# Two rotary half turns by DMA exchange in SBUF in place of permutation products, in a two-layer four-mixer block

## The reference, cut to what matters

```python
def apply_rope(x, cos, sin):
    half = cos.shape[-1]
    r = 2 * half
    ...
    x1, x2, rest = x[..., :half], x[..., half:r], x[..., r:]
    return jnp.concatenate([x1 * c - x2 * s, x2 * c + x1 * s, rest], axis=-1)
...
qb = apply_rope(qb, cos_p, sin_p) * DSWA_DH ** -0.5     # b, local attention
kb = apply_rope(kb, cos_p, sin_p)
...
qd = apply_rope(qd.reshape(B, S, RET_HEADS, RET_DK), cos_r, sin_r)    # d, retention
kd = apply_rope(kd.reshape(B, S, RET_HEADS, RET_DK), cos_r, sin_r) * RET_DK ** -0.5
```

## Time and profile before

| what | value |
|---|---|
| median of 3 runs (lowest, highest) | 2326.5 us (2324.55, 2334.76) |
| span of the profiled execution | 2324.0 us |
| TensorE busy | 2297.4 us, 99% |
| weight load of TensorE busy | 1870.2 us, 80% |
| VectorE, ACT, GpSimd busy | 851.0, 751.4, 1282.2 us |
| DMA | 196.72 MB, mean 85 GB/s |

### The profile page before, as it was taken

One profiled execution on the slowest core, in us unless ns is written; L12 is line 12 of the kernel. 1 busy time (PEld: TensorE's weight loads), 2 busy tenths in 40 slices (PEclk: granted clock), 3 DMA queues, 4 the chain that ended last, 5 costly groups with the idle time before them and its releaser, 6 DMA issues.

```text
span 2324.0 us, 31844 instructions
## 1 busy us (share of the span) xinstructions
PE 2297.4 (99%) x13054; PEld 1870.2 (80%) x13054; DVE 851.0 (37%) x1350; ACT 751.4 (32%) x1505; POOL 1282.2 (55%) x732
## 2 busy tenths in 40 slices
PE   8999999999999999999999999999999999999998
PEld 7788877877877888888887888778778778888887
DVE  4543225334445521123355430254243445112233
ACT  5633226213035321122355341451230544112121
POOL 5513654554554566677655136546555445666874
PEclk9999999999999999999999999999999999999999
DMA  4311331322221243322222113213222213333331
GB/s 151 91 38 47 95 87 46 118 82 86 75 89 52 92 124 92 100 94 97 82 79 85 36 54 93 73 60 115 84 88 84 74 60 101 108 100 94 97 100 64
DMA packets 105904, 196.72 MB, mean 85 GB/s; under 512 B 8480, under 2 KB 18848, under 8 KB 105504
## 3 DMA queue, kind: packets, MB, share of 16 engines
q1 hardware_dynamic: 104608, 188.40, 26.8%
q10 hardware_dynamic: 1152, 6.29, 0.8%
HBM read 192.57 MB, written 2.10 MB: 84 GB/s over the span
## 4 chain that ended last, share of the span: by engine, by line
PE 96%; ACT 2%; DVE 2%; issue 1%; DMA 0%; DVEq 0%; ACTq 0%
PE big L1722 71%; PE mix L1722 9%; PE mix L1867 5%; PE big L2074 1%; PE mix L2042 1%; PE mix L2144 1%; PE mix L2053 1%; PE mix L1827 1%; PE mix L2272 0%; PE mix L2225 0%; PE mix L1781 0%; ACT o_hi L618 0%; PE mix L2209 0%; PE mix L2195 0%; PE mix L1999 0%
## 5 line engine op out<-in xcount | busy, mean ns | idle before, releaser
L583 POOL TENSOR_TENSOR ring_lo<-stage,ring_hi 128x1024 fp32r<-128x1024 f32 (+3 forms) x364 | 912.4, 2507 | 30.4
L581 POOL TENSOR_SCALAR ring_hi<-stage 128x1024 fp32r<-128x1024 f32 (+3 forms) x364 | 371.3, 1020 | 987.9 <-PE big L1722 906.6
L1722 PE MATMUL big<-h_hi,ring_hi 128*128 128x512 f32 (+1 forms) x1888 | 720.6, 382 | 3.0 <-DVE h_lo L1173 1.8
L1722 PE MATMUL big<-h_hi,ring_lo 128*128 128x512 f32 (+1 forms) x1888 | 709.3, 376 | 0.0
L1722 PE MATMUL big<-h_lo,ring_hi 128*128 128x512 f32 (+1 forms) x1888 | 709.2, 376 | 0.0
L1722 PEld LDWEIGHTS big<-h_hi,ring_hi 128*128 128x128 f32 x1888 | 355.4, 188 | 75.1 <-issue 8.6
L1722 PEld LDWEIGHTS big<-h_lo,ring_hi 128*128 128x128 f32 x1888 | 355.4, 188 | 65.7
L1722 PEld LDWEIGHTS big<-h_hi,ring_lo 128*128 128x128 f32 x1888 | 355.7, 188 | 62.9 <-issue 1.4
L1663 DVE TENSOR_TENSOR h_lo<-scr,h_hi 128x1024 fp32r<-128x1024 f32 x64 | 84.7, 1323 | 248.5 <-ACT h_hi L1091 248.5
L1722 PE MATMUL big<-ring_hi,h_hi 128*128 128x512 f32 x448 | 174.2, 390 | 0.0
L1722 PE MATMUL big<-ring_lo,h_hi 128*128 128x512 f32 x448 | 174.1, 390 | 0.0
(11 more groups left out here) (304 smaller groups left out, 2758.0 us busy)
## 6 DMA issues: line engine op xcount, KB each, us to landing
stage<-in_w_in SPq DMA_DIRECT2D x168, 512.0 KB, 3.5
stage<-in_w_mlp_in SPq DMA_DIRECT2D x64, 512.0 KB, 3.7
stage<-in_w_mlp_out SPq DMA_DIRECT2D x64, 512.0 KB, 3.6
stage<-in_w_o SPq DMA_DIRECT2D x16, 512.0 KB, 3.6
stage<-in_w_br_a SPq DMA_DIRECT2D x8, 512.0 KB, 3.6
stage<-in_w_br_c SPq DMA_DIRECT2D x8, 512.0 KB, 3.6
stage<-in_w_br_d SPq DMA_DIRECT2D x8, 512.0 KB, 3.6
stage<-in_w_br_b SPq DMA_DIRECT2D x8, 512.0 KB, 3.6
```

The lines of the kernel that those rows point to most:

```text
L581: nc.gpsimd.tensor_scalar(rH[jw][0:pp, r, 0:kk, 0:job.n], w, 1.0, 0.0, ALU.mult, ALU.add).then_inc(sem("w_hi"), 1)
L583: nc.gpsimd.tensor_tensor(rL[jw][0:pp, r, 0:kk, 0:job.n], w, f32(rH[jw][0:pp, r, 0:kk, 0:job.n]), ALU.subtract).then_inc(sem("w_ready"), 1)
L1722: ins_ = MM(o_, a_, r_, start=s0, stop=s1)
```

## The change

Both rotations no longer use TensorE. The tiles are copied as they are to SBUF (`dX`, `bX`). `swapped` then issues four DMAs from ACT's queue which copy SBUF to SBUF, from `dX` to `dY` (four tiles at once, 32 rows each) and from `bX` to `bY` (8 rows each; bq0's four tiles at once, then bk0's, then bqk's one). They exchange the two halves of every head. The minus sign stands in the sine table. VectorE multiplies the copy by cosine, the exchanged copy by sine, and adds. In local attention the cosine product still reads the PSUM bank and frees it; the rows of `bY` that no DMA writes are zeroed once a layer by a memset on VectorE. `bX` and `bY` take the place of `o_hi` and `o_lo`. The matrices leave the constants, and the 13 rotations of a layer leave the order of the `mix` banks.

```diff
-        [... sel, rotation(8), rotation(32), -one(c <= p), ...], 1)
+        [... sel, -one(c <= p), ...], 1)
...
-        for b in (0, half):
+        for b, sign in ((0, -1.0), (half, 1.0)):
             cos[b:b + half] = np.cos(ang.astype(np.float64))
-            sin[b:b + half] = np.sin(ang.astype(np.float64))
+            sin[b:b + half] = sign * np.sin(ang.astype(np.float64))
...
+ROPE_LAST = (3, 7, 8)
+def rope_at(i):
+    return i % 4 if i < 8 else 4
...
+        o_at = nc.sbuf_base - 4 * 10 * S
+        b_raw = nc.alloc_sbuf_tensor_at("b_raw", [P, 10 * S], F32, offset=o_at)
-        dX, dY = sview(MB + 4096, 4), sview(MB + 10240, 2)
+        dX, dY = sview(MB + 4096, 4), sview(MB + 9216, 4)
+        bX, bY = (b_raw[:, 5 * S * i:5 * S * (i + 1)].rearrange("p (k w) -> p k w", w=S) for i in range(2))
...
+            def swapped(dst, src, tiles, half):
+                for b in range(0, P, DH):
+                    for r0, r1 in ((b, b + half), (b + half, b)):
+                        act.dma_start(dst[r0:r0 + half, tiles, :], src[r1:r1 + half, tiles, :]).then_inc(sem("exchanged"), 16)
...
             for i in range(4):
                 big_freed(act, ("dqk", i))
-                exact_hi(("drot", i), dX[:, i, :])
+            swapped(dY, dX, slice(0, 4), DH // 2)
...
-            def rope_hi(i):
+            def rope_raw(i):
                 ps = big_wait(act, WROPE[i])
-                if i >= 5:
-                    mix_wait(act, ("brot", i - 5))
-                A(oH[:, i % 5, :], ps[:, :], ACT.Copy).then_inc(sem("b_rhi"), 1)
+                if 4 <= i < 8:
+                    act.wait_ge(*upto("b_rope", i - 3))
+                A(bX[:, rope_at(i), :], ps[:, :], ACT.Copy).then_inc(sem("b_raw"), 1)
+                if i in ROPE_LAST:
+                    act.wait_ge(*upto("b_raw", i + 1))
+                    if i == 8:
+                        act.wait_ge(*upto("b_rope", 5))
+                    act.wait_ge(*upto("b_zero", 1))
+                    swapped(bY, bX, slice(0, 4) if i < 8 else slice(4, 5), 8)
...
             dve.wait_ge(*upto("tab", 16))
+            dve.wait_ge(*upto("exchanged", 64))
             for i in range(4):
-                rope(i, ("drot", i), ...)
+                TT(dX[:, i, :], dX[:, i, :], dTab[:, TRC:TRC + S], ALU.mult).then_inc(sem("d_rp"), 1)
+                TT(dY[:, i, :], dY[:, i, :], dTab[:, TRS:TRS + S], ALU.mult).then_inc(sem("d_rp"), 1)
+                dve.wait_ge(*upto("d_rp", 2 * i + 2))
+                TT(dQK[:, i, :], dX[:, i, :], dY[:, i, :], ALU.add).then_inc(sem("d_rope"), 1)
...
-            def rope_parts(i):
+            def rope_cos(i):
                 ps, key = big_wait(dve, WROPE[i]), WROPE[i]
-                dve.wait_ge(*upto("b_rhi", i + 1))
-                TT(oL[:, i % 5, :], ps[:, :], f32(oH[:, i % 5, :]), ALU.subtract).then_inc(sem("b_rlo"), 1)
+                dve.wait_ge(*upto("b_raw", i + 1))
                 if i >= 6:
-                    mix_freed(dve, ("brot", i - 6))
+                    dve.wait_ge(*upto("b_rope", i - 5))
                 big_free(TT(bR[:, i % 6, :], ps[:, :], bTab[:, 0:S], ALU.mult), key)
             def rope_sum(i):
-                key, t1 = ("brot", i), bR[:, i % 6, :]
-                ps = mix_wait(dve, key)
-                TT(ps[:, :], ps[:, :], bTab[:, S:2 * S], ALU.mult).then_inc(sem("b_rp"), 1)
+                t1, t2 = bR[:, i % 6, :], bY[:, rope_at(i), :]
+                dve.wait_ge(*upto("exchanged", 64 * (i // 4 + 2)))
+                TT(t2, t2, bTab[:, S:2 * S], ALU.mult).then_inc(sem("b_rp"), 1)
...
-            for i in range(4):
-                rope_parts(i)
-            for i in range(3):
-                rope_sum(i)
-                rope_parts(4 + i)
-            rope_sum(3)
-            rope_parts(7)
-            rope_sum(4)
-            rope_parts(8)
-            for i in range(5, 9):
-                rope_sum(i)
+            V.memset(b_raw[:, 5 * S:10 * S], 0.0).then_inc(sem("b_zero"), 1)
+            for first in (0, 4):
+                for i in range(first, first + 4):
+                    rope_cos(i)
+                for i in range(first, first + 4):
+                    rope_sum(i)
+            rope_cos(8)
+            rope_sum(8)
...
-            do("dv", between=d_rotate)
+            do("dv")
...
             do("bq0")
-            do("bk0", between=b_rotate)
+            do("bk0")
             do("bqk")
-            b_rotate(4)
-            do("bv", between=lambda i: b_rotate(5 + i))
+            do("bv")
...
-            mix_freed(pe, ("brot", 8))
+            pe.wait_ge(*upto("b_rope", 9))
```

More of the change, by code:

```diff
@@ L75 @@
 RING = 4
-CI, CTU, CLV, CMG0, CMG1, CMG2, CSEL, CRD, CRR, CNTL, CNTU, CNEG, CROW, CEND = np.cumsum(
-    [0, P, P, 6 * HB, 512, P, P, 2 * DH, P, P, P, P, 8, 16]).tolist()
-ROT = CEND - CRD
+CI, CTU, CLV, CMG0, CMG1, CMG2, CSEL, CNTL, CNTU, CNEG, CROW, CEND = np.cumsum(
+    [0, P, P, 6 * HB, 512, P, P, 2 * DH, P, P, 8, 16]).tolist()
+ROT = CEND - CNTL
 SCR = 20480
@@ L103, in shape_constants @@
         sel[h, h * DH:(h + 1) * DH] = 1.0
[L105 to L111, removed]
     consts = np.concatenate(
@@ L115, in shape_constants @@
          neg(np.concatenate([first, near], 1)), neg(c <= p),
-         neg((c <= p) & ((p - c) % 4 == 0)), sel, rotation(8), rotation(32), -one(c <= p), -one(c > p), -one(c + p >= 0)[:, 0:8], one(p % 32 == c)[:, 0:16]], 1)
+         neg((c <= p) & ((p - c) % 4 == 0)), sel, -one(c <= p), -one(c > p), -one(c + p >= 0)[:, 0:8], one(p % 32 == c)[:, 0:16]], 1)
     return np.ascontiguousarray(consts.astype(np.float32))
@@ L303, in mixer_keys @@
     k += [("an", h) for h in range(4)]
-    k += [("drot", i) for i in range(4)]
     for p in range(2):
@@ L308, in mixer_keys @@
             k += [("dpv", h), ("dn", h)]
-    k += [("brot", i) for i in range(9)]
     k += [("vt", q) for q in range(len(VT))]
@@ L327 @@
 MIX = number(mixer_keys(), 4)
-EXACT = [k for k in MIX if k[0] in ("drot", "dn")]
+EXACT = [k for k in MIX if k[0] == "dn"]
 PER_LAYER = {
@@ L1008, in scalar_layer @@
             for i in range(9):
-                rope_hi(i)
+                rope_raw(i)
             for t in range(4):
@@ L1582, in rope_sum @@
                 for r0, r1, out_, dil in parts:
-                    a, b_ = t1[r0:r1, :], ps[r0:r1, :]
+                    a, b_ = t1[r0:r1, :], t2[r0:r1, :]
                     if dil > 1:
@@ L1604, in vector_layer @@
                 if i == 0:
-                    mix_freed(dve, ("brot", 8))
+                    dve.wait_ge(*upto("b_rope", 9))
                 if i >= 3:
@@ L1874, in decays @@
                     for q in range(2):
-                        at = CROW - CRD + row + 2 * b + q
+                        at = CROW - CNTL + row + 2 * b + q
                         i = MM1(ps[:, 2 * P * q:2 * P * (q + 1)], rot_r[:, at:at + 1].to_broadcast((P, P)), g_rows[:, :])
@@ L2052, in stick_sums @@
                 for part in (c_H, c_L):
-                    MM(c_bank[u][:, :], rot_r[:, 2 * P:3 * P], part[:, u, :], start=False, stop=True, skip_group_check=True)
+                    MM(c_bank[u][:, :], rot_r[:, 0:P], part[:, u, :], start=False, stop=True, skip_group_check=True)
                     if u == 2:
                         o_ = c_bank[u][:, :].rearrange("p (e b c) -> p e b c", e=2, c=P)[:, :, 1, :]
-                        i = MM(o_, rot_r[:, 3 * P:4 * P], part[:, 0:2, 384:512], start=False, stop=True, skip_group_check=True)
+                        i = MM(o_, rot_r[:, P:2 * P], part[:, 0:2, 384:512], start=False, stop=True, skip_group_check=True)
                     elif u < 2:
-                        i = MM(c_bank[u][:, P:384], rot_r[:, 3 * P:4 * P], part[:, 2, 256 * u:256 * u + 256], start=False, stop=True, skip_group_check=True)
+                        i = MM(c_bank[u][:, P:384], rot_r[:, P:2 * P], part[:, 2, 256 * u:256 * u + 256], start=False, stop=True, skip_group_check=True)
                     else:
-                        i = MM(c_bank[u][:, P:], rot_r[:, 4 * P:4 * P + 1].to_broadcast((P, P)), part[:, u - 3, 0:384], start=False, stop=True, skip_group_check=True)
+                        i = MM(c_bank[u][:, P:], rot_r[:, 2 * P:2 * P + 1].to_broadcast((P, P)), part[:, u - 3, 0:384], start=False, stop=True, skip_group_check=True)
                 i.then_inc(sem("c_sum"), 1)
@@ L2149, in tensor_layer @@
             do("yd1")
-            def b_rotate(i):
-                ps = tile_of(("brot", i))
-                pe.wait_ge(*upto("b_rlo", i + 1))
-                MM(ps[:, :], rot_r[:, 0:P], oH[:, i % 5, :], start=True, stop=False)
-                done(MM(ps[:, :], rot_r[:, 0:P], oL[:, i % 5, :], start=False, stop=True), ("brot", i))
             do("bq0")
-            do("bk0", between=b_rotate)
+            do("bk0")
             do("bqk")
-            b_rotate(4)
-            do("bv", between=lambda i: b_rotate(5 + i))
+            do("bv")
             def values_natural(q):
```

51 lines of the change are left out of this document (12 added, 39 removed), and 12 rows, old and new, of the table PER_LAYER.

## The result

The changed kernel takes 2343.63 us in the median of 4 runs (2342.64 to 2349.12), the kernel before 2326.48. The ratio is 1.0069, with a 95% interval of 1.0047 to 1.0092: slower, by 0.69%. The profiled execution took 2342.64 us, its span is 2340.5, so 2.1 us lie around the span; the span before was 2324.0.

The account below looks back on a forecast made before the run. TensorE, busy 2297.4 of 2324.0 us, was taken as the bound. A layer: 13.0 stall + 1.7 clock - 6.1 rotations = +8.6 us, two layers +17.2, span 2341.2, plus 2.5 to the median: 2343.7 us, range 2331 to 2352.

Parts of the forecast that it names:

- part 1: TensorE loses 13 rotations a layer at 0.51 us each; 12 lie outside the stretch before bv's fourth tile, 6.1 us less.
- part 2: In retention, exchange and 12 VectorE operations take 43 us at worst, covered by 43.5 us until dg ends: no cost.
- part 3: bv's fourth tile waits for bqk's cosine product, now behind bk0's sums on VectorE: T + 13.3 unhindered, 3.2 us later.
- The landing: Arrival of bk0's exchanged tiles, for which VectorE's first sum waits: taken as T + 5, bounds T + 4.2 and T + 16.
- T: Start of bqk in local attention, 630.99 us in the first layer before; bv's fourth tile then started at T + 10.07.
- part 4: VectorE operations with two SBUF operands alternate with GpSimd's bv splits; TensorE resumes at T + 23.1, 13.0 us more a layer.
- Blind to the landing: The end of bv's wait hardly moves with the exchange's arrival: T + 7.5 gives 23.5, T + 10 23.8, T + 16 24.5.
- part 5: After the 13 us stall TensorE runs at a lower granted clock: 1.7 us lost a layer, bounds nothing and twice that.
- A: Rival: VectorE's operations keep today's length, TensorE's stall is 3.2 us more a layer, no clock loss, 2320.7 us; chance 0.10.
- C: Rival: bqk's bank comes free before bv's fourth tile wants it, TensorE keeps the whole gain, 2313.2 us; chance 0.04.
- D: Rival: the exchange lands later than T + 16, each us counting fully on both layers; T + 20 gives 2354; chance 0.06.
- B: Rival: VectorE gets several turns in a row or GpSimd is late, stall 5 to 8 us less, 2326 to 2337; chance 0.08.

Follow-up runs that it names:

- experiment 1: The changed kernel with `rope_cos(8)`, bqk's cosine product, issued ahead of the four `rope_sum` of bk0: 2316.8 us, ratio 0.9943 to the kernel before.
- experiment 6: The kernel before with the retention half of the change alone, local attention keeping its permutation products: 2324.38 us, ratio 0.9987.
- experiment 5: The changed kernel with only the first of bk0's four tiles exchanged, 16 KB per DMA in place of 64 KB: 2347.92 us, ratio 1.0081.
- experiment 2: The changed kernel with sine table and sine product in PSUM, so no local rotation operation reads two SBUF operands: 2331.64 us, ratio 1.0013.

## Why the prediction was right, point by point

The path that the prediction names is the one that the runs show. That the time, 2343.6 beside 2343.7, is so close is luck in part: the steps err in both directions.

- **What leaves TensorE** (part 1): right, also in its size. GpSimd's splits start at TensorE's pace, and during bk0 they show what a rotation cost, before and after (bqk's small units are split while bk0 runs):

```profile
613.71 0.40 POOL L581 TENSOR_SCALAR ring_hi<-stage 128x256 fp32r<-128x256 f32 x1 [2.38 <-PE big L1722]
619.66 0.40 POOL L581 TENSOR_SCALAR ring_hi<-stage 128x256 fp32r<-128x256 f32 x1 [4.72 <-PE big L1722]
...
610.89 0.41 POOL L582 TENSOR_SCALAR ring_hi<-stage 128x256 fp32r<-128x256 f32 x1 [1.91 <-PE big L1711]
616.33 0.75 POOL L582 TENSOR_SCALAR ring_hi<-stage 128x256 fp32r<-128x256 f32 x1 [4.21 <-PE big L1711]
```

They are 5.95 us apart before and 5.44 after: 0.51. In experiment 1 all 13 rotations of a layer bring the splits 6.35 us forward, 12.7 in two layers; its span is 12.4 us shorter.
- **Retention costs nothing** (part 2): right. VectorE was done some 20 us before dg ended, and the half alone gives 4.3 us (experiment 6), beside 8 x 0.51 = 4.1.
- **The place and the cause of the wait** (part 3): right, and shown by experiment 1, in which only the place of one instruction differs from the changed kernel. The fourth tile of bv waits for the bank of bqk, in both layers.
- **The landing** (part 3): mis-sized. I took T + 5, it was T + 9.2. An issue of such a DMA takes ACT 0.63 us, where the earlier trace rows have 0.36, and the fourth lands 6.4 us after its issue (5.9 in the second layer), where the 128 KB load of the earlier trace rows has 2.1. The sum left out that weights are loaded at the same time: the same transfer for bq0, with less beside it, landed some 2.4 us sooner (experiment 5). These are the DMAs of local attention (durations in ns, least, median, most):

```profile
L699 ACTq DMA_DIRECT2D b_raw<-b_raw x24: 631/632/1197, 605.7 to 1801.1; - x24
```

- **The exclusion** (part 4): right as a mechanism, and its size depends on the landing. I had nine operations in turn with three units of GpSimd; because of the late landing only the first four met GpSimd in the first layer. It is 5.4 us of the first stall (experiment 2). The Trainium skill, SBUF - State Buffer, section "Who interferes with whom", states that a VectorE instruction with two SBUF inputs contends with a GpSimd one that reads SBUF, that the shared ports are an exclusive lock, and that the order of issue decides who blocks. The trace agrees (2.71 and 1.48 us against 0.69 and 1.05), and experiment 2, with one SBUF operand each, shows no lengthening.
- **Blind to the landing** (part 4): right, and the reason why a landing that came 4.2 us late did no harm. With the sums starting at T + 1.5, T + 7.4 and T + 9.2 the cosine product ended at T + 20.95, T + 22.35 and T + 22.62; I had 23.0 for T + 5. By the rule of the Trainium skill, SBUF - State Buffer, section "Door 1: The DMA port swizzle", I had estimated a landing near T + 8, closer to T + 9.2 than my T + 5. But that estimate is made of bytes alone, and with a quarter of the bytes 4.55 and 3.21 us of the 6.39 and 5.91 were left.
- **The clock** (part 5): right in kind, too small. 2.7 us a layer, not 1.7: the low clock held for 5.9 us of work behind the first stall and 5.3 behind the second, not for 3.4. I also wrote that TensorE had stood idle long only at the start, and took the low clock for a matter of the start. The profile before had low stretches, too, near 740 and 1890 us, at the end of local attention, where TensorE is busy throughout. They are in both kernels; the first costs the same in both, the second does not:

```profile
1885.00:1906.00 21.00, 21.00 (x76) 13.18 (x74) 7.55 (x11) 10.04 (x10) 8.28 (x6) 0.84 0.18 54
...
1901.00:1922.00 21.00, 21.00 (x83) 14.05 (x83) 10.52 (x14) 11.30 (x13) 7.67 (x5) 0.92 0.21 66
```

The first line is of the kernel before, the second of the changed one. 21 x 0.08 = 1.7 us.
- **The sum.** Measured: +12.5 for the stretch (22.67 and 22.4 less 10.07), +2.7 for the clock, less 12 x 0.51 = 6.1: +9.1 a layer, 18.2 in two, where I had 8.6 and 17.2. The starts of GpSimd's splits fall back by 9.5 us in the first layer and 9.0 in the second. The span grew by 16.5, because the second low stretch just named takes 1.7 us more before than after. The mis-sized terms are the clock (1.0 a layer too small) and the stretch (0.5 too large), together 1.0 too small in two layers; with the 1.7 us, on which I had not counted, the span came out 0.7 below the forecast. The median of the runs lies 3.1 us above this profiled span, where I had 2.5, and that closes the gap. The start is no part of it: there the column says 0.66 before and 1.00 after for 15 to 20 us, but in both kernels products start 0.21 us apart for some 3 us, and the splits behind it differ by 0.3.
- **The rivals.** A (no exclusion) fell with the operations' lengths; C (no stall) would have needed the order of experiment 1; D (a landing later than T + 16) did not happen. B asked for a stall 5 to 8 us shorter; it was 0.4 and 0.7 shorter than forecast, and VectorE got no turns in a row while GpSimd had work.

## What to carry to other kernels

Look for the instruction that frees what another engine waits for, and issue it before the work that only needs to be done sometime: 52 products taken from the engine that bounds were worth 12 us at the same clock, and one such instruction, behind four sums, turned that into a loss of 17. An operand moved from PSUM to SBUF made a VectorE operation up to four times as long beside a busy GpSimd (0.69 to 2.87 us); that matters only where somebody waits for it, so first find out who does. A wait behind which the clock is low costs more than its length, here 2.7 us on 12.8. Filling it brought that back at the place, but not in the whole.

## What the runs showed of the hardware that I had not expected

- A DMA between 8 partitions of SBUF and 8 others takes its issuing engine 0.63 us (0.36 for the table loads over 128 partitions), and the last of four lands 4.55 and 3.21 us after its issue with 16 KB, and 6.39 and 5.91 with 64 KB, beside weight loads. With 64 KB and less DMA traffic (76 GB/s in place of 195) it landed some 2.4 us sooner.
- The granted clock was 0.70 over the 12.9 us wait and 0.50 for 5.9 us of products behind it; behind a wait of 7.4 us (experiment 2) it was low for 5.3 us.
- Executions of one kernel differ by the clock that they are granted: the delta rule of the second layer has 14 to 17 us at half rate in four of the ten profiles and none in the others, and the 37 runs of the kernel before spread by 12 us, from 2324.8 us at 0.997 to 2337.0 at 0.992. The runs have to be matched by it before differences of a few us are read.
